# A layer in fp32 halves: both planes of the activations `h` get 16 columns of room behind each tile

## The reference

```
h  = rmsnorm(x, g_mix_pre);  z = h @ w_in
A  = silu(group_layernorm(causal_dwconv(glu(z), width 31)))
B  = mlstm_chunkwise(q, k, v, i, f) with per-head LayerNorm and sigmoid o-gate
x += rmsnorm(concat(A, B) @ w_out)
up = causal_dwconv(rmsnorm(x) @ w_up, width 3)
x += rmsnorm((gelu(up[:, :2816]) * up[:, 2816:]) @ w_down)
x += (p @ w_ple) * sigmoid(rmsnorm(x) @ w_ple_gate)
```

## Time and profile before

| | us |
|---|---|
| median of 3 runs | 2688.59 |
| lowest and highest run | 2686.04, 2690.0 |
| the profiled execution's own time | 2685.84 |
| its span (first to last instruction) | 2684.0 |
| TensorE busy | 2655.4 |
| VectorE busy | 1726.9 |
| ScalarE busy | 921.4 |

### The profile page before, as it was taken

One profiled execution on the slowest core, in us unless ns is written; L12 is line 12 of the kernel. 1 busy time (PEld: TensorE's weight loads), 2 busy tenths in 40 slices (PEclk: granted clock), 3 DMA queues, 4 the chain that ended last, 5 costly groups with the idle time before them and its releaser, 6 DMA issues.

```text
span 2684.0 us, 37676 instructions
## 1 busy us (share of the span) xinstructions
PE 2655.4 (99%) x14541; PEld 2581.4 (96%) x14541; DVE 1726.9 (64%) x3699; ACT 921.4 (34%) x1932; POOL 237.1 (9%) x180
## 2 busy tenths in 40 slices
PE   9999999999999999999999999999999999999999
PEld 7989999999999999999999999999999998899998
DVE  7985898865566666555675664756866636472645
ACT  5464434464332122344321233542112425311113
POOL 4433515140000000000000000000000000000000
PEclk9999999999999999999999999999999999999999
DMA  9867999877566666565666666466666575466665
GB/s 331 321 222 293 359 335 365 315 282 285 188 233 233 233 234 234 216 239 210 227 233 233 234 234 256 182 226 233 229 233 232 216 284 146 179 240 229 235 233 204
DMA packets 125117, 660.59 MB, mean 246 GB/s; under 512 B 22010, under 2 KB 22654, under 8 KB 55182
## 3 DMA queue, kind: packets, MB, share of 16 engines
q1 hardware_dynamic: 111150, 628.29, 63.8%
q10 hardware_dynamic: 13792, 29.92, 3.3%
HBM read 533.04 MB, written 125.11 MB: 245 GB/s over the span
## 4 chain that ended last, share of the span: by engine, by line
PE 93%; DVE 4%; ACT 2%; DMA 1%; issue 1%; SPq 0%; DVEq 0%; ACTq 0%
PE proj L732 85%; PE m L732 1%; PE m L899 1%; PE m L932 1%; PE m L933 1%; PE m L893 1%; PE m L910 0%; PE m L761 0%; DMA w_split<-w_kept 0%; DVE small L1994 0%; PE m L952 0%; PE m L705 0%; PE m L704 0%; PE m L706 0%; PE m L865 0%
## 5 line engine op out<-in xcount | busy, mean ns | idle before, releaser
L732 PE MATMUL proj<-h_split,w_split 128*128 128x416 f32 x8112 | 1562.8, 352 | 4.5 <-DVE h_split L1831 2.1
L732 PEld LDWEIGHTS proj<-h_split,w_split 128*128 128x128 f32 x8112 | 1505.7, 188 | 20.1 <-issue 7.8
L732 PE MATMUL proj<-f_split,w_split 128*128 128x416 f32 x4584 | 880.8, 352 | 7.7 <-DMA w_split<-w_kept 2.2
L732 PEld LDWEIGHTS proj<-f_split,w_split 128*128 128x128 f32 x4584 | 851.5, 188 | 28.1 <-DVE f_split L2042 4.4
L1874 DVE SCALAR_TENSOR_TENSOR cv<-a_ext,vecs,cv 128x416 f32<-128x416 f32 (+1 forms) x480 | 302.5, 677 | 0.0
L1536 ACT ACTIVATE temp_room<-proj 128x416 f32<-128x416 f32 x176 | 91.3, 519 | 547.4 <-PE proj L732 547.3
L688 POOL TENSOR_TENSOR w_split<-w_raw,w_split 128x512 fp32r<-128x512 f32 x174 | 234.3, 1368 | 368.2 <-ACT w_split L1112 368.2
L2346 DVE SCALAR_TENSOR_TENSOR m<-temp_room,vecs,m 128x416 f32<-128x416 f32 (+1 forms) x440 | 256.8, 652 | 0.0
L2376 DVE TENSOR_TENSOR f_split<-m,f_split 128x416 fp32r<-128x416 f32 x110 | 65.1, 592 | 233.4 <-ACT f_split L1548 233.4
L2343 DVE TENSOR_SCALAR m<-temp_room,vecs 128x416 f32<-128x416 f32 (+1 forms) x220 | 145.9, 709 | 65.6 <-ACT temp_room L1536 65.5
L1750 DVE TENSOR_TENSOR mix_room<-mix_room,temp_room 128x416 f32<-128x416 f32 x131 | 81.0, 618 | 102.9 <-ACT temp_room L1130 97.2
(11 more groups left out here) (288 smaller groups left out, 1975.0 us busy)
## 6 DMA issues: line engine op xcount, KB each, us to landing
w_split<-w_kept SPq DMA_DIRECT2D x430, 1024.0 KB, 4.8
w_kept<-w_split SPq DMA_DIRECT2D x107, 1024.0 KB, 6.5
w_raw<-in_w_units SPq DMA_DIRECT2D x216, 256.0 KB, 4.7
x_resid<-in_x ACTq DMA_DIRECT2D x5, 1664.0 KB, 12.0
out_y<-x_resid ACTq DMA_DIRECT2D x8, 832.0 KB, 8.6
rows<-in_x ACTq DMA_DIRECT2D x4, 832.0 KB, 7.4
w_raw<-in_x ACTq DMA_DIRECT2D x3, 832.0 KB, 9.0
qkv<-in_p ACTq DMA_DIRECT2D x5, 416.0 KB, 5.9
```

The lines of the kernel that those rows point to most:

```text
L732: ins = mm(to, home[:, low_w, b * P:b * P + P], act[:, n, low_a, :], start=n == 0 and not low_w and not low_a, stop=n == len(blocks) - 1 a ...
```

## The change

`ROOM` becomes a pair, one value for each plane. The high tiles start 1728 bytes apart in place of 1792, the low ones 1728 in place of 1664. `h_split` grows by 16 columns, so all tensors behind it start 64 bytes further on; `f_room` stays. The instructions, their order, their shapes and their waits stay as they are.

```
-ROOM = 32
+ROOM = (16, 16)
...
-        h_room = sb("h_split", [P, (KD - 1) * (T + ROOM) + T + KD * T], F32R)
-        h = Tiles(h_room, [k * (T + ROOM) for k in range(KD)], [(KD - 1) * (T + ROOM) + (k + 1) * T for k in range(KD)])
+        h_low = KD * (T + ROOM[0])
+        h_room = sb("h_split", [P, h_low + (KD - 1) * (T + ROOM[1]) + T], F32R)
+        h = Tiles(h_room, [k * (T + ROOM[0]) for k in range(KD)], [h_low + k * (T + ROOM[1]) for k in range(KD)])
```

## The result

The change made the kernel slower: 2700.39 us in the median of 6 runs (2698.76 to 2709.43) against 2688.39 us (2684.23 to 2691.24) for the kernel before, a ratio of 1.0051 with a 95% interval of 1.0037 to 1.0065. That is +12.0 us, where the forecast had +5.7.

The account below looks back on a forecast made before the run. TensorE's matmul count times spacing was taken to bound the kernel. Spacing on `h` rising 0.8 ns over 7700 matmuls gave 6.2 us, 5.7 on the chain, hence a forecast median of 2694.3 us, range 2684 to 2706.

Parts of the forecast that it names:

- Only the spacing can act: TensorE's matmuls on `h` and `f`: time is their number times spacing; a nanosecond on each of 8208 is 8.2 us.
- High tiles, +1.3 ns: High tiles, 2/3 of matmuls on `h`: pitch 1792 to 1728 loses their evenness, spacing 186.7 to 188.0 ns.
- the sum: Both planes of `h`: mean spacing 187.2 to 188.0 ns, +0.8 ns on 7700 matmuls, 6.2 us, 5.7 us on the chain.
- Low tiles, -0.2 ns: Low tiles, 1/3 of matmuls on `h`: one changing offset pattern for another, spacing 188.2 to 188.0 ns.
- Everything behind moves by 64 bytes: Tensors behind `h_split`, weights included: no change for matmuls on `f`, bounds 0.3 ns either way on 4704, 1.4 us.
- The top of the range, 189.4 ns of the `f` stage: Worst spacing seen on `f` applied to every matmul on `h`: 18 us more, giving 2706 us.
- The reason, offsets within 256 bytes: Matmul streams run evenly at 186.7 ns if start offsets within 256 bytes stay fixed; varying offsets give 187.8 to 189.4.
- Room helps: Rival: 16 columns of room make low tiles of `h` as even as high ones, -4.1 us, 2684.5 us; chance 0.18.
- Odd multiples of 64 are dear in themselves: Rival: `h` tiles starting at odd multiples of 64 bytes cost 6.7 ns on average, +55 us, 2744 us; chance 0.12.
- No change: Rival: mean spacing on `h` stays at 187.2 within 0.2 ns, 2687 to 2690 us; chance 0.13.
- A shorter load or a later stall: Weight loads: slower landing would show first on `f`, where TensorE waited 2.2 us in all; nothing was counted.

Follow-up runs that it names:

- e9: Kernel before with only the high tiles moved to 1728 bytes apart; low tiles, size of `h_split` and everything behind stay: 2694.76 us, ratio 1.002.
- e2: Changed kernel with 48 idle columns behind `h_split`, so everything behind starts 256 bytes further on than in the kernel before: 2692.96 us, ratio 1.0015 to the kernel before.
- e1: Kernel before with its old tiles, everything behind `h_split` 64 bytes further on: 2697.9 us, ratio 1.0034.
- e5: Kernel before with the weights (`w_split`, `wg_split`) 64 bytes further on and everything behind them 256 bytes on: 2699.85 us, ratio 1.0047.
- e3: Kernel before with high and low tiles of `h` alternating without room, 3328 bytes apart in each plane, nothing behind moved: 2695.14 us, ratio 1.0023.
- e7: Kernel before with 16 idle columns ahead of `f_room`, so tiles and weights all start 64 bytes further on together: 2688.82 us, ratio 1.0002.
- second profiles: Kernel before and changed kernel each executed and profiled once more, unchanged: 2688.23 us and 2698.99 us.
- e10: Kernel before with old `h` tiles, `h_split` 64 bytes further on and everything behind it 256 bytes on: 2691.98 us, ratio 1.0013.

## Why the prediction was right in direction and short in size

- *Only the spacing can act.* Right. Counts, waits and the other engines stayed; the cost lies in the busy time of the two groups at one line.
- *High tiles, +1.3 ns.* The loss of evenness came (346/350/354 in place of 349/349/350), and the size was near in e9, where only they moved: 1.0 ns as a mean over both planes, at most 1.6 per high matmul. In the change itself the `h` stages rose by 2.8 and 1.7 ns over both planes, against the +0.8 of the sum. For the tiles alone, without the shift (e2), the sum had +5.7 us: the times say +4.0 us (1.6 to 6.5), the busy time 10.6.
- *Low tiles, -0.2 ns.* Mis-sized, with the wrong sign: 349/352/355, against 344/351/353. Eight low ones take 932.78 - 931.26 = 1.52 us, 190 each, against the 188.0 that was taken.
- *Everything behind moves by 64 bytes: no change, at most 1.4 us.* This is the step that failed. Its own experiments are e1 and e5, +9 and +12 us. On `f` the page says 3.8 us for the change and 8.1 for e1 against a bound of 1.4, and the term had no share for `h`, which pays in e1's first stage as well (189.2 against 187.2). The bound of 0.3 ns had no row behind it: I argued that a stream that is uneven already can't get worse.
- *The top of the range, 189.4 ns of the `f` stage.* Misread: that stretch holds two pauses (starts 398 and 294 ns apart at 877.7 us), and without them it is at 188.2. It was no worst spacing, and the change's first `h` stage reached 190.0.
- *The reason, offsets within 256 bytes.* Refuted by e3. The earlier trace rows show that places matter where room can't, and this stands; they don't show which relation. Each of them has the weights' places in it as well as the tiles', and I read the tiles' alone; e7 and e5 show that the weights' count too. So the reason given for the direction does not hold, and most of the time came from the term put at nothing: that 2700.4 us lies on the forecast side and in the range of 2684 to 2706 is in part luck.
- *The rivals.* Room helps: refuted, by the change itself and by e3. Odd multiples of 64 are dear in themselves: refuted by e7, where all tiles and `w_split` start at such. No change: refuted.
- *A shorter load or a later stall.* None; the loads' waits on `f` are 2.1 us in both second profiles.
- The Trainium skill's rule of N / 2.4 GHz + about 2.5 ns ("TensorE: Matmul & The Clock Gate", section "Wait - 56ns, not 53.3ns?") has no term for places and would have had no change; these runs range from 186.7 to 190.0 ns for one shape on `h`. The same page of the Trainium skill, section "Step-by-step: what each phase is for", says that loading the next weights takes no read bandwidth from the running matmul, having a port of its own. No run here shows ports, but e7 against e5 shows that the two streams are not indifferent to each other's places.

## What to carry to other kernels

Where TensorE streams without a stop, a pad of 64 bytes anywhere between two operands is a change to be timed, even behind the tensors that it was meant for: here it cost 9 us alone, of 12 for the whole. To keep an experiment on one tensor's layout clean, fill it up to the old size, or shift all operands together; a shift of everything by 64 bytes was free here. A stage's row repeated to 10 ns between two executions of one kernel, so a single profile's stage rows tell what five rounds of times barely do. Read all stages, though: the last `f` stage went the other way, and in e1 the first `f` stage is at 190.7 ns in block 1 and 190.2 in block 2.

## What the runs showed of the hardware

- For 416 columns in the `float32r` type the mean spacing of an `h` stage was between 186.7 ns, as much as 448 cycles at the granted 2.4 GHz, and 190.0 ns, by the places of tiles and weights. 186.7 is no floor: eight low tiles of e1 ran evenly at 184. bf16 matmuls of the same width stood at 177.
- The spacing is not set by the two operands alone. In the kernels e1 and e5 the two `h` stages read the same tiles and the same ring slots in the same order (they begin with units 40 and 73, both slot 1), and one has 189.2, the other 186.7, in both kernels. This came up in the three kernels whose `f` was off by 64 (e1, e5, the change) and in none of the others (at most 0.2 ns between the two stages), e10 included, whose `h` was off by 192 while `f` was not. The last `f` stage says the same from the other side: same tiles, same weights, 193.6 in e1 and 189.6 in the change. That the stream carries something over from the stage before is a guess; no run here tests it.
- What the relation is stays open. On the first `f` stage 0, 128 and 256 bytes more were alike and 64 dearer; on the last one 64 was dearer in e1 and e5 and cheaper in the change; on `h` none of 64, 128 and 192 repeats another.
- Two executions of one program differ by short stretches at the lower granted clock: 0.50 from 722 to 724 us in the changed kernel's first execution, behind 2.00 us without a matmul, and none there in its second.
